# FFN input half of a decoder trunk: two pairs of feature tiles at a time as a two-level block product

## What is computed

```
def swiglu_ffn(x, w_in, w_out):
    g, u = jnp.split(x @ w_in, 2, axis=-1)
    return (jax.nn.silu(g) * u) @ w_out

for i in range(DEPTH):                      # DEPTH = 2
    ...
    xp = xp + swiglu_ffn(rmsnorm(xp, norm2_w[i]), ffn_w_in[i], ffn_w_out[i])
    xs = xs + swiglu_ffn(rmsnorm(xs, norm2_w[i]), ffn_w_in[i], ffn_w_out[i])
```

## Time and profile before

| | |
|---|---|
| time, median of 3 runs | 4056.01 us (4053.74 to 4058.81) |
| span of the profiled execution | 4056.7 us, 0.7 above that median |
| instructions | 54763 |
| TensorE busy in that span | 3810.3 us, 94% |
| mean granted TensorE clock | 0.975 of full |
| the input half's pairs, second layer | 3205 to 3744 us of the span |

### The profile page before, as it was taken

The page is one execution under the profiler, slowest core; times in us unless marked ns, Lnnn a source line. Parts: engine busy times, 40 slices in busy tenths (PEclk is TensorE's granted clock), DMA queues, the critical chain, the costliest instruction groups (busy, mean ns, idle before and its releaser), DMA issues. The chain is left out here.

```text
span 4056.7 us, 54763 instructions
## 1 busy us (share of the span) xinstructions
PE 3810.3 (94%) x20290; PEld 2938.6 (72%) x20290; DVE 1802.1 (44%) x2980; ACT 944.4 (23%) x2138; POOL 1208.6 (30%) x1021
## 2 busy tenths in 40 slices
PE   8999989998799999999999898989989999999999
PEld 5666666666686888878867766666657688888887
DVE  4565456654453111136661216666655411112666
ACT  3333332333210000000001005656531100000001
POOL 0111011111142333324341105656533233332432
PEclk9999999999699999999999999999989999999999
DMA  4010101101132111123331220000033111112322
GB/s 148 28 42 26 37 27 42 38 26 38 55 93 76 41 41 39 38 82 105 93 127 32 74 77 19 1 2 1 1 95 94 65 41 41 41 41 58 114 86 80
DMA packets 322017, 223.99 MB, mean 55 GB/s; under 512 B 28442, under 2 KB 313235, under 8 KB 319827
## 3 DMA queue, kind: packets, MB, share of 16 engines
q1 hardware_dynamic: 316164, 214.99, 17.9%
q0 software_dynamic: 2048, 5.25, 0.4%
q10 hardware_dynamic: 3650, 1.64, 0.2%
HBM read 191.54 MB, written 34.37 MB: 56 GB/s over the span
## 5 line engine op out<-in xcount | busy, mean ns | idle before, releaser
L775 PE MATMUL ps<-xT,work 128*128 128x272 f32 x2688 | 643.4, 392 | 0.0
L775 PEld LDWEIGHTS ps<-xT,work 128*128 128x128 f32 x2688 | 510.7, 190 | 105.3
L1311 PE MATMUL ps<-xn,work 128*128 128x363 f32 (+1 forms) x1536 | 549.4, 477 | 7.6 <-issue 7.4
L775 PE MATMUL ps<-xn,work 128*128 128x272 f32 x2016 | 489.9, 392 | 3.9 <-DVE work L846 3.9
L775 PEld LDWEIGHTS ps<-xn,work 128*128 128x128 f32 x2016 | 382.9, 190 | 83.9 <-issue 5.1
L387 PE MATMUL ps<-work 128*128 128x272 f32 x1676 | 404.3, 398 | 13.4 <-PEq L1146 7.3
L387 PEld LDWEIGHTS ps<-work 128*128 128x128 f32 x1676 | 321.8, 193 | 84.4 <-issue 17.0
L2936 POOL TENSOR_SCALAR work<-work 128x640 f32<-128x640 f32 (+4 forms) x192 | 313.9, 1645 | 196.7 <-DVE work L2839 196.4
L1311 PEld LDWEIGHTS ps<-xn,work 128*128 128x128 f32 x1536 | 261.2, 192 | 105.1 <-issue 21.8
L648 POOL TENSOR_TENSOR xT<-xT,work 128x272 f32<-128x272 f32 x96 | 198.6, 2081 | 252.2 <-DVE work L512 163.6
L2022 POOL TENSOR_TENSOR xT<-xT,consts 128x512 f32<-128x512 f32 x96 | 124.8, 1314 | 441.6 <-DVEq L1851 379.7
(11 more groups left out here) (425 smaller groups left out, 5855.2 us busy)
## 6 DMA issues: line engine op xcount, KB each, us to landing
work<-in_ffn_w_in_dram SPq DMA_DIRECT2D x88, 512.0 KB, 5.0
xn<-in_ffn_w_out_dram SPq DMA_DIRECT2D x46, 704.0 KB, 4.5
work<-in_gdn_w_in_dram SPq DMA_DIRECT2D x32, 512.0 KB, 4.2
work<-in_ffn_w_out_dram SPq DMA_DIRECT2D x18, 704.0 KB, 4.5
ffn_parked_residual<-xT SPq DMA_DIRECT2D x2, 4352.0 KB, 13.7
work<-in_gdn_w_out_dram SPq DMA_DIRECT2D x32, 256.0 KB, 2.9
work<-in_nsa_w_out_dram SPq DMA_DIRECT2D x64, 128.0 KB, 2.9
xT<-ffn_parked_residual SPq DMA_DIRECT2D x4, 1632.0 KB, 10.2
```

Of the source, the lines that this page charges most:

```text
L775: ins = pe.matmul(acc(a, n), w[:, k, :], t[:, k, a * SUB:(a + 1) * SUB], start=(first and k == 0), stop=(k == HK - 1), skip_group_check=True)
L1311: mm = pe.matmul(unit_acc(u, m), w[j % 2][:, k, :], c.xn[:, k, o:o + cnt], start=(k == 0), stop=(k == KD - 1))
```

## The change

The input half is rebuilt; pair 1 stays a one-level product, and the other 20 pairs are taken two at a time, as ten quads. A quad's blocks are twice as wide (two feature tiles), and its seven outer products are each done once more as a 2 x 2 block product with seven inner products: blocks of 2 K-tiles, 128 features and 272 tokens, two matmuls each. That makes 49 inner products of two matmuls per quad.

- **Tokens.** VectorE makes four inner mixes (544 elements) of each of the seven outer token operands once a layer; they lie in the room of hidden tiles and of part of `xn`.
- **Outer weights.** GpSimd makes `s1` to `s4` of a quad (`sums`, two instructions of 512 elements each); weights come from DRAM as eight transfers of 256 KB a quad.
- **Inner weights.** GpSimd makes four sums of 256 elements for each outer product (`inner_weights`), double-buffered over outer products.
- **Results.** Each outer product is taken out into a buffer X of 2 x 544 elements (one of six) by two copies on ScalarE and five additions on VectorE. VectorE then adds whole outer products (1088 elements, seven a quad, `add`), ScalarE takes Silu of 1088 elements twice a quad (`gate`), GpSimd multiplies (`hidden`, four instructions of 544 a quad).
- **Parking.** The second token half's hidden tiles all go to DRAM (544 KB a quad) and come back in one transfer in the output half, where steps 4 and later use them. The first token half's of quads 0 to 4 go to DRAM too and come back in four transfers during the last quad.
- The quads are written out, not looped.

The core of the diff (the SyncE part, the one-level pair's code and the semaphores' names are cut):

```diff
@@ out_stage
+                    if n % PAIRS == 0 and arrived:
+                        pe.wait_ge(*arrived[n // PAIRS])
                     step(n)
@@ ffn_stages, tensor
+                def inner(a, n, w, t, first):
+                    for k in range(2):
+                        ins = pe.matmul(acc(a, n), w[:, k, :], t[:, k, :], start=(first and k == 0), stop=(k == 1), skip_group_check=True)
+                    ins.then_inc(pm, 1)
...
+                    pe.wait_ge(ws, 4 * q + 4)
...
+                        pe.wait_ge(cv, 2 * (q - 2) + 2)
+                        pe.wait_ge(ext, 5 * (q - 2) + 5)
+                    inner(s, 0, block_of(w, 0, 0), tokens_block(j, 0, 0), True)
+                    inner(s, 1, w2, m2, True)
+                    inner(s, 2, w3, m3, True)
+                    inner(s, 3, w1, m1, True)
+                    pe.wait_ge(cv, 2 * q + 1)
+                    inner(s, 0, block_of(w, 0, 1), tokens_block(j, 1, 0), False)
+                    pe.wait_ge(ext, 5 * q + 2)
+                    inner(s, 2, block_of(w, 1, 1), m4, False)
+                    pe.wait_ge(ext, 5 * q + 3)
+                    inner(s, 3, w4, tokens_block(j, 1, 1), False)
@@ ffn_stages, scalar
+                for q in range(NQ):
+                    s = q % 2
+                    place_free(q)
+                    act.wait_ge(pm, INNER * q + 1)
+                    act.activation(X(q, 1, 0), acc(s, 0), ACT.Copy).then_inc(cv, 1)
+                    if q and (q - 1) % OUTER in (1, 6):
+                        gate(q - 1)
+                    act.wait_ge(pm, INNER * q + 5)
+                    act.activation(X(q, 0, 0), acc(s, 0), ACT.Copy).then_inc(cv, 1)
+                gate(NQ - 1)
@@ ffn_stages, vector
+                dve.wait_ge(mixed, 4)
+                for j in range(3):
+                    for n in (1, 2, 4):
+                        mix_tokens(j, n)
                 dve.wait_ge(umm, 1)
...
+                for q in range(NQ):
+                    if q:
+                        extract(q - 1, 5)
+                        combine(q - 1)
+                    for n in range(1, 4):
+                        extract(q, n)
+                    if q:
+                        combine_late(q - 1)
+                    if q in (0, 1, 2):
+                        mix_third((4, 5, 6)[q])
+                    extract(q, 4)
+                extract(NQ - 1, 5)
+                combine(NQ - 1)
@@ ffn_stages, gpsimd
+                def inner_weights(q):
...
+                    if q >= 2:
+                        pool.wait_ge(pm, INNER * (q - 2) + 7)
+                    w = weights[g][role[j]]
+                    a11, a12, a21, a22 = [block_of(w, r, x) for r in range(2) for x in range(2)]
+                    w1, w2, w3, w4 = f.sigma[q % 2]
+                    pool.tensor_tensor(w1, a21, a22, ALU.add).then_inc(ws, 1)
+                    pool.tensor_tensor(w3, a11, a21, ALU.subtract).then_inc(ws, 1)
+                    pool.wait_ge(ws, 4 * q + 1)
+                    pool.tensor_tensor(w2, w1, a11, ALU.subtract).then_inc(ws, 1)
+                    pool.wait_ge(ws, 4 * q + 3)
+                    pool.tensor_tensor(w4, a12, w2, ALU.subtract).then_inc(ws, 1)
...
+                for q in range(NQ):
+                    g, j = divmod(q, OUTER)
+                    if j == 2:
+                        sums(g, 3)
+                    if q + 1 < NQ:
+                        inner_weights(q + 1)
+                    if j == 0:
+                        sums(g, 2)
+                    elif j == 1 and g:
+                        hidden(g - 1, True)
+                    elif j == 3:
+                        sums(g, 4)
+                    elif j == 5:
+                        hidden(g, False)
+                    elif j == 6 and g + 1 < QUADS:
+                        sums(g + 1, 1)
+                hidden(QUADS - 1, True)
@@ first_back
+        sp.wait_ge(late_st, 16 * QUADS)
+        sp.dma_start(hid3[:, 2:KF, HT:NT], park1).then_inc(late_back_, 16)
```

More of the change, by code:

```diff
@@ L464, in mix @@
                     b11, b12, b21, b22 = [rhs[:, k, tokens(n, half)] for k in (lo, hi) for half in range(2)]
+                    if which == 1 and n % PAIRS == 0 and arrived:
+                        dve.wait_ge(*arrived[n // PAIRS])
                     if which == 1:
@@ L752, in _ @@
+                sp.wait_ge(gmm, 1)
                 sp.wait_ge(umm, 1)
[L753 to L762, removed]
@@ L767, in _ @@
+                for r in (1, 2):
+                    ow.load(sp, out_w, 0, r)
+                store_late(last)
             @block.tensor
@@ L798, in _ @@
                 pe.wait_ge(prod, 2)
[L799 to L802, removed]
+                one_level()
+                for q in range(NQ):
+                    outer(q)
             @block.scalar
             def _(act):
-                act.sem_inc(av, 6)
                 act.wait_ge(summed, 1)
@@ L824, in _ @@
[L824 to L827, removed]
-                for a in range(2):
-                    part(PAIRS - 1, a)
+                for a in range(2):
+                    act.wait_ge(mm1, 7 * a + 1)
+                    act.activation(p1[a], acc(a, 0), ACT.Copy).then_inc(av1, 1)
+                    act.wait_ge(mm1, 7 * a + 5)
+                    act.wait_ge(dv1, 5 * a + 1)
+                    act.activation(p1[a], acc(a, 0), ACT.Silu).then_inc(av1, 1)
+                    act.wait_ge(dv1, 5 * a + 5)
+                    act.activation(hid_at(1, 1, a), hid_at(1, 1, a), ACT.Silu).then_inc(av1, 1)
@@ new lines, in hidden @@
+                def hidden(g, late):
+                    q = OUTER * g
+                    if late:
+                        pool.wait_ge(sl, 2 * g + 2)
+                        out, a, b = X(q + 6), X(q + 6), X(q + 3)
+                    else:
+                        pool.wait_ge(sl, 2 * g + 1)
+                        pool.wait_ge(oa, 7 * g + 4)
+                        out, a, b = X(q + 4), X(q + 1), X(q + 4)
+                        if g >= SPILLED:
+                            out = hid3[:, 2 + 2 * g:4 + 2 * g, 0:HT]
+                    for r in range(2):
+                        pool.tensor_tensor(out[:, r, :], a[:, r, :], b[:, r, :], ALU.mult).then_inc(hp, 1)
```

409 lines of the change are left out of this document (325 added, 84 removed).

## The result

| | before | changed |
|---|---|---|
| time, median of 4 runs each | 4057.41 us (4053.74 to 4060.15) | 3949.79 us (3944.61 to 3951.59) |
| span of the profiled execution | 4056.7 us | 3949.9 us |
| ratio of the times | | 0.9736, 95% interval 0.9722 to 0.9749 |

The account below looks back on a forecast made before the run. TensorE was taken to bound the kernel, 539.00 us of 539.00 busy in the input half. Per layer -64.2 + 6.3 + 0.7 + 4.2 + 1.5 + 1.0 = -50.5, two layers -101: 4056 to 3955 us, range 3945 to 3972.

Parts of the forecast that it names:

- The products: Input half: 140 matmuls fewer a layer at 0.458 us, -64.2 us a layer; groups of two matmuls cost nothing.
- GpSimd's list: GpSimd's work in a quad: 42.5 of 44.9 us; TensorE waits 0.7 us before the fourth outer product, +6.3 a layer.
- five-product stretch: Sixth product to next quad's fourth: GpSimd needs 32.7 to 32.9 us against TensorE's 32.1.
- The port: SBUF port shared by VectorE and GpSimd, an exclusive lock: each two-SBUF-input addition costs GpSimd 1.0 us.
- rival 2: GpSimd bounds the whole half: 256 elements at 0.80 us gives 3982, at 0.925 gives 4027; chance 0.22.
- Start: Before the pairs: nine token mixes of 544 elements delay TensorE's first product, +0.7 us a layer.
- end: Step from input to output half: chain after TensorE's last product takes 6.5 us against 2.3, +4.2 a layer.
- clock: Output half's first 22 records, 6.97 us, slower after longer idle; bounds 0 and 3.1, +1.5 a layer taken.
- transfers: Output half: late hidden tiles (5440 KB) returning delay weights for step 1; bounds 0 and 5, +1.0 a layer.
- Rival 1: Quads of the input half: GpSimd keeps up and TensorE never waits; 3937 to 3943 us; chance 0.20.
- the second one below: Without the port lock GpSimd's sum in a quad would be 35.5 us and TensorE would never wait.
- Rival 3: VectorE's additions wait for two GpSimd instructions, delaying extractions: +3 us a layer, 4062; chance 0.08, shared with anything beyond 4048.

Follow-up runs that it names:

- e1: Changed kernel with a quad's late hidden product (1088 elements) made by VectorE in one instruction instead of two of GpSimd's; 3931.88 us, 44.9 us a quad.
- e4: Changed kernel without the fourth inner weight sum of each outer product, 7 GpSimd sums fewer a quad; 3937.1 us, 44.9 us a quad.
- e7: Changed kernel with one more GpSimd sum of 256 elements in the third outer product's set of quads 1 to 9; 3960.3 us, 46.38 us a quad.
- e2: Changed kernel with one extra VectorE instruction a quad, 1088 elements, both inputs in SBUF, result unchanged; 3992.6 us, mostly 47.69 us a quad.
- e3: Changed kernel with three more VectorE extractions a quad (0.44 us each), one operand in PSUM; 3949.8 us, 45.7 us a quad.
- e8: Changed kernel with two more GpSimd sums of 256 elements in the third outer product's set of quads 1 to 9; 4009.1 us.

## Why the prediction was right

**The products.** 140 matmuls fewer a layer at 0.458 us, and no price for groups of two matmuls: quads without waits are 44.9 us (e1, e4), as worked out.

**GpSimd's list.** The wait is where it was put, before the fourth outer product, ended by the engine that was named, nine times, and 0.77 a quad where 0.7 was taken (6.9 us a layer for 6.3). The five-product stretch took 32.9 us (45.69 less two products of 6.42), where 32.7 to 32.9 was worked out. The price of 256 and 544 elements from the line is right to 0.01 us. That it is GpSimd is shown by three runs: less on its list and the wait is gone (e1, e4), one sum more and it grows by that sum (e7). GpSimd is 87% busy over the half, with its blocked time, not about 93% as I wrote; that figure was one of a whole quad, and there it is 92% (41.99 of 45.70 us from 1349.3 on); the pair of the first 26 us, where GpSimd is busy 35%, takes the half's figure down.

**The port.** 1.0 us for each addition: with one beside it L1220 took 1.77 where it takes 0.72, and the mean over all additions is 1.04. That it hangs on where the operands lie is shown by e2 against e3. What the prediction lacked is the step: how much a delay of GpSimd costs depends on whether the sum that TensorE waits for starts before or after VectorE's next addition. The changed kernel's sum starts 0.85 us ahead of it. Past that, 0.9 (e8) to 1.1 us (e2) come on top; rival 2's table with 1.8 us a layer for each 0.01 us was therefore too cheap from 0.04 us (0.85 over 20) upwards. At 0.80 us for 256 elements GpSimd would have been 1.5 us a quad later, as with e8's two sums, and the time nearer to e8's 4009 than to the 3982 of the table; this is an estimate, no run has such an instruction.

**Start, end, clock, transfers.** Start: TensorE's wait there is 2.35 us in the changed kernel; before, it was 1.95:

```profile
1258.72 2.10 PE L775 MATMUL ps<-xn,work 128*128 128x272 f32 x8 [1.95 <-DVE work L846]
```

From the end of VectorE's last mix of the outer tokens to TensorE's first product it is 8.12 us (1250.60 to 1258.72), and was 7.71 (from 1251.01). So 0.4 for 0.7. End: TensorE's idle is 6.68 for 2.13, +4.6 for 4.2. (The prediction has the last product's end before at 1797.8; by the earlier trace rows, 1800.11 less 2.13, it is 1797.98.) Clock: the first 22 records took 7.77 and 7.75 for 6.97, +0.8 for 1.5; the output half is 0.8 us longer as a whole (287.73 for 286.95, to the start of its last addition), so this is all of it, and the term for transfers is 0.0 where I took 1.0. That the clock's term is +0.8 has luck in it: behind the same idle of 6.7 us the 22 records took 6.74 in e8 and 8.25 in e7, so -0.2 to +1.3 could have come.

**The sum.** The products with the waits are 482.1 - 539.3 = -57.2; -57.2 + 0.4 + 4.6 + 0.8 = -51.4 a layer, -103 in two, against -101. The sum is closer than its terms: waits and end were 0.6 and 0.4 too low, start, clock and transfers 0.3, 0.7 and 1.0 too high. The profiled spans differ by 106.8. The remaining 4 us are in stretches that the change doesn't touch, the second mixer above all, where TensorE waited 5.4 us for the cache's rows in place of 8.1, and which moved by as much from one run to another. From the start of the first output half to the next pairs, whose mixer code is the same in all these kernels, it took between 1398.3 us (e8) and 1402.2. No run ties these 4 us to the change; their cause was not looked for.

**Rivals.** Rival 1 (no wait) was 7 us a layer from true, and e1 and e4 make it true; its own terms give 3939 to 3942, not 3937 to 3943, and e4 measured 3937. It is also the case that the prediction calls the second one below, where it speaks of the sum without a lock. Rival 3 (VectorE waits for two GpSimd instructions) didn't occur: the longest addition took 2.187 us, 0.90 over its 1.28, so at most the rest of one instruction, and TensorE waited for no extraction.

## What to carry to other kernels

An algorithm that saves matmuls pays in additions, so the forecast is made on the engine that adds: list its instructions between two of its sync points, price them by size from the trace, add the price of every instruction of VectorE with two SBUF inputs that falls beside them (1.0 us for one of 1.28 here), and compare with TensorE's time over the same stretch, not over the whole round; here 95% over a quad was 102% over five of its seven products. When that is over by a little, moving one piece of work to an empty place of the other engine takes away the whole wait (e1: 2.6 us a quad moved, 18 us won in all, of which 14 are the waits). And look how far the awaited instruction is from the next one that would take the port: beyond that distance a small delay costs far more than itself (1.0 us cost 2.0 in e2, 1.4 cost 2.3 in e8), before the clock's part.

## What the hardware showed that I had not expected

- What a delay of GpSimd costs has a step in it: 0.69 us more on GpSimd cost 0.69 a quad, 1.4 us cost 2.28, and 1.0 us by way of an addition cost 2.0.
- The same idle of TensorE doesn't always lose the clock. Behind waits of 2.8 us it held in 4 of 18 quads and fell in 14 (e8), behind waits of 2.5 us it held in 16 and fell in 2 (e2), and behind those of 0.5 to 1.2 us it never fell (changed kernel, e3, e7). Idle of 2.1 us at the output half took it down before the change (0.59).
- In the output half's first product the length of the idle says little of what the lower clock costs. The 22 records took 6.97 us behind 2.1 us of idle, 6.8 to 8.0 behind 5.3, and 6.7 to 8.3 behind 6.7.
